# Half-width products in the triangular inverses of a chunked RWKV-7 recurrence, with 32-row operands at the last level

## What is computed

```
def step(S, inp):
    r_t, w_t, k_t, v_t, a_t, b_t = inp
    sa = jnp.einsum('bhvk,bhk->bhv', S, a_t)
    S = S * w_t[:, :, None, :] + sa[..., None] * b_t[:, :, None, :] + v_t[..., None] * k_t[:, :, None, :]
    y = jnp.einsum('bhvk,bhk->bhv', S, r_t)
    return S, y
```

## Time and profile before

| what | us |
|---|---|
| median of 3 runs (2051.44 to 2052.02) | 2051.97 |
| the profiled execution, its own time | 2048.59 |
| its span, first to last instruction | 2046.5 |
| TensorE busy (matmul records) | 1983.2 |
| VectorE busy | 1164.9 |
| ScalarE busy | 784.8 |
| GpSimd busy | 170.1 |
| mean granted TensorE clock | 0.99 |

### The profile page before, as it was taken

How to read it: one execution, slowest core, us unless ns; L and a number is a source line. 1 busy time by engine, 2 the same in 40 slices (tenths; PEclk the granted TensorE clock), 3 DMA queues, 4 the chain that set the end, 5 groups by cost and what they waited for, 6 DMA issues and landing times.

```text
span 2046.5 us, 35345 instructions
## 1 busy us (share of the span) xinstructions
PE 1983.2 (97%) x14436; PEld 1610.0 (79%) x14436; DVE 1164.9 (57%) x1781; ACT 784.8 (38%) x1384; POOL 170.1 (8%) x130
## 2 busy tenths in 40 slices
PE   6999999989999999998999999999999999999997
PEld 2777799977787878776777877877888878888885
DVE  5689765667534343567566657475564266556423
ACT  6777333334322122346632222134343244434311
POOL 1000222210202020100002022020000010000001
PEclk9999999999999999999999999999999989999999
DMA  5321000032232323230144544543541122332421
GB/s 192 116 88 47 2 4 4 8 143 93 87 109 93 94 92 102 77 111 22 48 157 170 183 155 143 185 157 113 181 125 34 62 83 93 100 96 91 144 93 41
DMA packets 61003, 201.47 MB, mean 98 GB/s; under 512 B 8000, under 2 KB 11200, under 8 KB 59584
## 3 DMA queue, kind: packets, MB, share of 16 engines
q1 hardware_dynamic: 60096, 192.93, 28.3%
q10 hardware_dynamic: 768, 6.55, 1.0%
HBM read 190.68 MB, written 6.42 MB: 96 GB/s over the span
## 4 chain that ended last, share of the span: by engine, by line
PE 71%; issue 17%; DVE 8%; ACT 2%; POOL 2%; DMA 0%; DVEq 0%; POOLq 0%; SPq 0%; ACTq 0%
PE bank L2015 17%; PE bank L2017 17%; PE bank L2016 17%; POOL HS L2807 2%; PE bank L2229 1%; PE bank L2197 1%; PE bank L2244 1%; PE bank L2201 1%; DVE wlo L1242 1%; DVE HR L1602 1%; DVE GBZ L1419 1%; PE bank L2495 1%; PE bank L2481 1%; PE bank L2516 1%; PE bank L2649 1%
## 5 line engine op out<-in xcount | busy, mean ns | idle before, releaser
L1242 DVE TENSOR_TENSOR wlo<-raw,whi 128x1024 fp32r<-128x1024 f32 x270 | 327.5, 1222 | 572.6 <-ACT whi L693 571.0
L693 ACT ACTIVATE whi<-raw 128x1024 fp32r<-128x1024 f32 x270 | 282.3, 1057 | 708.6 <-PE bank L2017 693.1
L2015 PE MATMUL bank<-inh,whi 128*128 128x512 f32 x1200 | 470.5, 392 | 1.8 <-DVE inl L1479 1.6
L2017 PE MATMUL bank<-inh,wlo 128*128 128x512 f32 x1200 | 467.0, 389 | 0.0
L2016 PE MATMUL bank<-inl,whi 128*128 128x512 f32 x1200 | 467.0, 389 | 0.0
L2015 PEld LDWEIGHTS bank<-inh,whi 128*128 128x128 f32 x1200 | 225.2, 188 | 57.7 <-issue 6.3
L2017 PEld LDWEIGHTS bank<-inh,wlo 128*128 128x128 f32 x1200 | 225.2, 188 | 47.3
L2016 PEld LDWEIGHTS bank<-inl,whi 128*128 128x128 f32 x1200 | 225.3, 188 | 46.8 <-issue 0.7
L2015 PE MATMUL bank<-hidh,whi 128*128 128x512 f32 x576 | 228.5, 397 | 8.3 <-DVE HR L1602 5.6
L2017 PE MATMUL bank<-hidh,wlo 128*128 128x512 f32 x576 | 224.5, 390 | 0.0
L2016 PE MATMUL bank<-hidl,whi 128*128 128x512 f32 x576 | 224.3, 389 | 0.0
(11 more groups left out here) (424 smaller groups left out, 2831.9 us busy)
## 6 DMA issues: line engine op xcount, KB each, us to landing
raw<-in_mlp_w SPq DMA_DIRECT2D x128, 512.0 KB, 3.6
ADW<-in_w_ada SPq DMA_DIRECT2D x32, 768.0 KB, 5.2
raw<-in_w_up SPq DMA_DIRECT2D x44, 512.0 KB, 3.5
raw<-in_w_in SPq DMA_DIRECT2D x28, 512.0 KB, 3.7
raw<-in_a_w_rkv SPq DMA_DIRECT2D x24, 512.0 KB, 3.5
raw<-in_w_down SPq DMA_DIRECT2D x22, 512.0 KB, 3.5
raw<-in_a_wo SPq DMA_DIRECT2D x8, 512.0 KB, 8.0
raw<-in_b_wq SPq DMA_DIRECT2D x8, 512.0 KB, 3.4
```

The lines of the kernel that those rows point to most:

```text
L693: act.activation(whi[u % SLOTS][:, :], raw[u % SLOTS][:, :], ACT.Copy).then_inc(w_hi, 1)
L1242: dve.tensor_tensor(lo[:, :], r[:, :], h[:, :].bitcast(F32), ALU.subtract).then_inc(w_lo, 1)
L2015: pe.matmul(o, w[:, wc], xh, start=start, stop=False)
L2017: return pe.matmul(o, r[:, wc], xh, start=False, stop=stop)
```

## The change

The correction that a level adds to Z is zero except in the columns of the second block of each pair of blocks. The changed kernel computes these columns alone. Of the 64 columns of a head it takes the 32 later ones (runs of 2, 4, 8, 16 and at the last level 32 columns, each 2 << lv long), and writes them packed side by side in the bank, 256 columns for the 8 blocks instead of 512. The copy is 128x256, and the add reads 256 packed columns and updates the 256 columns of Z in their strided places. At the last level Q also uses a quarter of the stationary matrix alone: rows 32 to 63 and columns 0 to 31 of each head, and z takes 32 rows of `TI` and `QS`. The number of products, copies, adds, transposes and waits is as before.

```
+        def later(ap, lv):
+            return ap.rearrange("p (a two b) -> p a two b", two=2, b=2 << lv)[:, :, 1, :]
+        def later_all(ap, lv):
+            return ap.rearrange("p c (a two b) -> p c a two b", two=2, b=2 << lv)[:, :, :, 1, :]
+        def part(ap, lv):
+            return ap.rearrange("p (a b) -> p a b", b=2 << lv)
+        def part_all(ap, lv):
+            return ap.rearrange("p (c a b) -> p c a b", c=CB, b=2 << lv)
...
-                        act.activation(QS[x][:], pairs(PB[x][:]), ACT.Copy).then_inc(ai.sem, ai.step(("q", g, lv, x)))
+                        act.activation(QS[x][:, :, 0:HC // 2], pairs(PB[x][:, 0:CB * HC // 2]), ACT.Copy).then_inc(ai.sem, ai.step(("q", g, lv, x)))
...
-                        dve.tensor_tensor(z, z, pairs(PB[2 + x][:]), ALU.add).then_inc(di.sem, di.step(("z", g, lv, x)))
+                        zl = later_all(z, lv)
+                        dve.tensor_tensor(zl, zl, part_all(PB[2 + x][:, 0:CB * HC // 2], lv), ALU.add).then_inc(di.sem, di.step(("z", g, lv, x)))
...
+            def narrow(cb):
+                return slice(cb * HC // 2, (cb + 1) * HC // 2)
...
-                                mm = pe.matmul(PB[x][hs, tok(cb)], LM[x][lv % 2][hs, cb, :], GBZ[j % 4][hs, cb, HC:P], start=True, stop=True)
+                                if lv < LEVELS - 1:
+                                    mm = pe.matmul(part(PB[x][hs, narrow(cb)], lv), LM[x][lv % 2][hs, cb, :], later(GBZ[j % 4][hs, cb, HC:P], lv), start=True, stop=True)
+                                else:
+                                    lo, hi = slice(HD * h, HD * h + 32), slice(HD * h + 32, HD * h + 64)
+                                    mm = pe.matmul(PB[x][lo, narrow(cb)], LM[x][lv % 2][hi, cb, 0:32], GBZ[j % 4][hi, cb, HC + 32:P], start=True, stop=True)
...
-                                mm = pe.matmul(PB[2 + x][hs, tok(cb)], TI[x][hs, cb, :], QS[x][hs, cb, :], start=True, stop=True)
+                                ks = hs if lv < LEVELS - 1 else slice(HD * h, HD * h + 32)
+                                mm = pe.matmul(PB[2 + x][hs, narrow(cb)], TI[x][ks, cb, :], QS[x][ks, cb, 0:HC // 2], start=True, stop=True)
```

## The result

The changed kernel takes 2065.76 us (median of 4 runs, 2063.32 to 2068.85) where the kernel before takes 2051.70 (4 runs, 2050.97 to 2052.02): a ratio of 1.0071, 95% interval 1.0059 to 1.0084, so 14 us slower. I had forecast 8 us faster.

What follows compares the result with a forecast made beforehand. TensorE, busy 97% of the span, was taken as the bound, with waits for adds between inverse levels; 7.4 + 0.4 + 0.3 = 8.1 us off the 2051.97 median gave 2043.9 us, range 2037 to 2052.

Steps and rivals of the forecast that it cites:

- the clock falls: slower: Rival for the inverses: TensorE's granted clock drops with the half-wide products and the kernel gets slower; chance 0.08.
- the rest: Leftover chance 0.06: a TensorE stall like that in the last pair comes out longer or shorter with the new timing.
- The adds: VectorE's adds in the inverses: 0.69 to 0.42 us each, two in the chain, 0.54 us less per joint.
- the second rival: Adds do not shrink because of short runs: 2048 if at the two lowest levels, 2051 if at all; chance 0.10.
- The level of 3.74 us: One inverse level, 4.27 us before: TensorE's four phases of 0.93 would run without a gap.
- The products: Levels 0 to 3: weight loads set the pace, so phases stay at 0.93 us; rival that they shrink, chance 0.12.
- the half-way case: Products in the inverses shrink half-way towards half their phase time: 2038 us; most of that rival's 0.12.
- The strided reading: Rival: TensorE's strided reads of Z slow Q, 2050 with one slow level, 2056 with two; chance 0.06.
- The last level: Last level of each inverse: shorter Q gains 1.7 us, shape switches cost 1.3, net gain 0.4 us.
- that switch: Going from Q to z at the last level changes the array's shape, priced at 0.18 us a switch.
- The sum: Total forecast gain: 7.4 from joints, 0.4 from last levels, 0.3 at the last pair's end, 8.1 us.
- the joints: Places between levels of the inverses where adds hold TensorE: 14 at 0.53 us each, 7.4 us gained.

Runs made afterwards that it cites:

- E2: Changed kernel with 64-row operands at the last level, 32 moving columns everywhere: 2062.03 us, 1.0043 of the kernel before.
- E8: E2 with the transfers that start at the end of the third recurrence put off to the end of the last inverse: 2056.37 us, ratio to before 1.0014.
- E12: E6 with a stall made in each pair by doing one transpose behind level 1 three times: 2048.76 us, 0.9991 of the kernel before.
- E1: Changed kernel with only the narrow adds kept, products and copies of full width, 64-row operands: 2046.34 us, 0.9973 of the kernel before.
- E11: E2 with a stall made in each pair by doing one transpose behind level 1 three times: 2086.66 us, 1.0184 of the kernel before.
- E3: Changed kernel with full-width products at levels 0 to 3, last level still 32 columns on 32-row operands: 2050.42 us, 0.9994 of the kernel before.
- E6: Changed kernel with Q streaming the later columns twice, z streaming the full copy's 64, 64-row operands: 2045.46 us, 0.9968 of the kernel before.
- E5: Changed kernel with full-width products (64 columns, 64-row operands) in the last pair of chunks alone: 2052.48 us, 1.0006 of the kernel before.

## Why the prediction was wrong, point by point

**The step that failed** is the rival "the clock falls: slower", to which I gave 0.08. I had seen what speaks for it, a TensorE busy with one-column products whose granted clock was 0.70 from 1656.80 to 1660.20. I put it aside with this: "with 54 records in 3.61 us, its width still 64, the clock stayed at 1.00", and the half-wide phases would do "somewhat more". That was one stretch of full-width products with a stall in it, compared with a level of half-wide products without one. The case that decides, both at once, was not in my comparison, though the rows of that very stretch showed that stalls occur there and the sentence on "the rest" of the chances spoke of them. The runs put in its place: half-wide products alone keep the clock at 1.00 (pairs 0 and 2 of E2), and keep it over stalls of up to 0.63 us (last pair of E8); full-width products keep it over a stall of 1.4 us (E12) and get it back behind one of 2.5 us, after 3.4 us at 0.51 (E1); half-wide products with a stall of 0.92 us (E2) or 1.3 (E11) lose it (0.50) and do not get it back while they go on. At the last level, with two narrowings at once, it falls to 0.50 with no stall over 0.23 us in the nine microseconds ahead of it (pairs 0 to 2 of the changed kernel, 1 and 2 of E3). In pair 1 of the changed kernel there is none at all in that time.

**Its price** I had estimated as all or nothing: every phase at twice its time, a level of 7.5 us, some 60 us for all 20 levels. In the changed kernel the four falls sum to 51 us (3 x 6.8 + 30.7). If all that TensorE does there took twice its time, 26 us would be lost; against E6, which has none, the loads behind the last recurrence start at 464.71 instead of 443.42, 21.3 us later. E6 in turn is 5.7 us ahead of the kernel before (449.12), which leaves the 15.6 of the section on the result. A phase did not double either: at a clock of 0.50 two take 3.41 us instead of 1.87, and a level 6.8. That a fall over about an eighth of the inverses would already eat the 8 us was a sound estimate; the falls cover far more than that.

**The adds** were right: 0.42 for 0.69, the runs of 2 included, so the second rival has no part. The level of 3.74 us with VectorE out of the chain was right as well, and that TensorE's own four phases would be what is left.

**The products** were right: streaming does not set the pace, which is 0.0292 us a record with 32 columns as with 64. No run shows the 2038 us of the half-way case, which my range takes in: the phases of the changed kernel take the 0.93 us that they took before. The strided reading costs nothing: the phases of E6 and of the changed kernel read Z in such runs and take 1.87 us for two, no longer than those of E1, which do not (1.86 to 1.87).

**The last level.** Its two Q phases take 1.26 us together where I had 1.02, so the 32-column operands bring less than their loads alone suggest:

```profile
320.14 1.26 PEld L2254 LDWEIGHTS bank<-GBZ,LM 32*32 32x32 f32 x64
320.25 0.42 DVE L1436 TENSOR_TENSOR GBZ<-GBZ,bank 128x256 f32<-128x256 f32 x1
...
321.44 2.98 PEld L2270 LDWEIGHTS bank<-QS,TI 32*64 32x64 f32 x64
```

and z starts 0.04 behind the end of Q instead of 0.11 before it, so that switch costs 0.15, for my 0.18. What the last level is worth at full clock can be read in pair 2 of E3, where the clock falls only at 373.3: from z of the level below (367.54) to the scores (372.98) it takes 5.44 us against three times 1.87, 0.17 less. Over four pairs that is 0.7, so my net 0.4 was about right for what is next to nothing.

**The sum.** The 8.1 us are 6.2 in E6 and 5.0 in E1, which leave the last level as it was. Where no stall falls, the joints are worth what I said: from its first to its last weight load the inverse of pair 1 takes 18.75 us in E6 and 20.88 before, 2.13 less, for four joints of 0.53. In the pairs 0 and 2 it is 1.60 and 0.94 less. There E6 has stalls of 0.27 to 0.38 us in which TensorE waits for nothing that the profile shows, one in pair 0 and three in pair 2, where the kernel before has one in each (0.20 and 0.28), and here and there two phases take up to 2.1 us instead of 1.87. Before, the wait for the adds (0.54 us at a joint) could absorb such delays; in a level without slack each shows. How much of the missing 2 us is theirs was not measured apart. The chain of E6 has between 249 and 434 us

```profile
408.70 1.92 issue
415.25 0.93 issue
```

in the last pair, beside 1.94 and 0.66 before. I had named such stalls as a risk of 0.06 without putting them into the sum.

## What to carry to other kernels

Before you halve what a matmul streams, look in the trace whether its weight load is the longer of the two. Here it was: two phases took 1.87 us with 64 columns and with 32, so the narrowing won no time on TensorE, and what was won lay on the engine that adds (0.69 to 0.42 us an add; the copies, 0.60 to 0.38, were no link of the chain). I would make these narrow and leave the products wide. And judge the clock with what will interrupt the phase: a stall of 1.39 us left wide products at a clock of 1.00 (E12), one of 1.33 us put narrow ones at 0.50 for 20.5 us, to the end of the inverse, and the profile called TensorE busy for 20.50 of these 20.50 us (E11).

## What the runs showed of the hardware that I had not expected

- A TensorE that the profile calls busy for 23.90 of 23.90 us, both in matmuls and in weight loads, ran at a granted clock of 0.50 all that time (E2). Its loads were slower too, 3.63 us for 64 of them instead of 1.95 to 2.0, so phases that wait for their loads took 1.8 times as long.
- Streaming the same columns a second time, for nothing, made the kernel 16.6 us faster than E2 without the repeat (2045.46 against 2062.03).
- TensorE's unexplained stalls in the last pair follow the transfers: 2.5 us in its inverse with them there, 2.5 us in the recurrence when they were moved there. That its instructions come late because of the transfers is the likely reason; it was not measured apart.
- How much of the clock is lost differs from run to run of the same kernel: E5 has runs from 2047.92 to 2060.96 us with mean clocks of 0.987 and 0.982, E8 from 2044.59 to 2057.95 with 0.990 and 0.982. Why a given run escapes was not settled.
